# Inverting a chunk's triangular matrix in a hybrid decoder layer: 16x16 diagonal blocks by substitution on VectorE, three levels instead of six, two slots for each hop

## The reference

```python
lower = jnp.where(strict, jnp.einsum('bhnid,bhnjd->bhnij', kb, k) * decay, 0.0)
eye = jnp.eye(c, dtype=jnp.float32)
tmat = lax.linalg.triangular_solve(eye + lower, jnp.broadcast_to(eye, lower.shape),
                                   left_side=True, lower=True, unit_diagonal=True)
u = tmat @ vb
w = tmat @ (kb * jnp.exp(g)[..., None])
```

## Time and profile before

| what | value |
|---|---|
| median of 3 runs | 823.94 us (823.16 to 825.99) |
| the profiled execution's own time | 824.77 us |
| its span, first to last instruction | 823.1 us |
| TensorE busy | 807.9 us |
| VectorE busy | 484.0 us |
| ScalarE busy | 410.0 us |
| GpSimd busy | 140.5 us |
| mean granted TensorE clock | 0.995 of full |

### The profile page before, as it was taken

The page is one execution under the profiler, slowest core; times in us unless marked ns, Lnnn a source line. Parts: engine busy times, 40 slices in busy tenths (PEclk is TensorE's granted clock), DMA queues, the critical chain, the costliest instruction groups (busy, mean ns, idle before and its releaser), DMA issues.

```text
span 823.1 us, 12564 instructions
## 1 busy us (share of the span) xinstructions
PE 807.9 (98%) x3859; PEld 666.3 (81%) x3859; DVE 484.0 (59%) x794; ACT 410.0 (50%) x641; POOL 140.5 (17%) x222
## 2 busy tenths in 40 slices
PE   8899999999999999999999999999999999999996
PEld 7788887888888888878888888888888888888874
DVE  4666448555754664585458456654764566765563
ACT  4564545545544555454545545454555563444441
POOL 9112112110211021102112110211031100001120
PEclk9999999999999999999999999999999999999999
DMA  8856565565656455746565564556454566578652
GB/s 210 231 138 190 139 186 156 172 174 158 178 151 179 129 178 153 193 138 180 152 178 162 153 186 136 180 160 185 137 171 137 183 212 187 182 237 282 196 155 102
DMA packets 179207, 142.15 MB, mean 173 GB/s; under 512 B 10880, under 2 KB 144240, under 8 KB 179056
## 3 DMA queue, kind: packets, MB, share of 16 engines
q1 hardware_dynamic: 179184, 141.85, 59.6%
HBM read 139.72 MB, written 2.10 MB: 172 GB/s over the span
## 4 chain that ended last, share of the span: by engine, by line
PE 91%; DVE 3%; issue 2%; SPq 2%; DMA 1%; ACT 0%; DVEq 0%; POOLq 0%; POOL 0%; ACTq 0%
PE pj L497 27%; PE pj L499 27%; PE pj L498 26%; PE dn_ps L569 1%; PE dn_ps L574 1%; PE dn_ps L552 1%; PE dn_ps L539 1%; DVE w_lo L1011 1%; SPq L269 1%; DVE decay L1100 1%; PE dn_ps L564 1%; DMA w_raw<-in_w_in_dram 1%; SPq L274 1%; SPq L252 1%; PE mo_ps L547 0%
## 5 line engine op out<-in xcount | busy, mean ns | idle before, releaser
L1011 DVE TENSOR_TENSOR w_lo<-w_raw,w_hi 128x1024 fp32r<-128x1024 f32 x251 | 312.9, 1250 | 179.9 <-ACT w_hi L785 179.0
L497 PE MATMUL pj<-w_hi,xt_hi 128*128 128x512 f32 x860 | 356.9, 415 | 3.2 <-DVE w_lo L1011 3.1
L785 ACT ACTIVATE w_hi<-w_raw 128x1024 fp32r<-128x1024 f32 x251 | 264.3, 1058 | 149.9 <-PE pj L499 132.2
L499 PE MATMUL pj<-w_hi,xt_lo 128*128 128x512 f32 x860 | 338.7, 394 | 0.0
L498 PE MATMUL pj<-w_lo,xt_hi 128*128 128x512 f32 x860 | 336.4, 391 | 0.0
L499 PEld LDWEIGHTS pj<-w_hi,xt_lo 128*128 128x128 f32 x860 | 161.8, 188 | 36.6
L497 PEld LDWEIGHTS pj<-w_hi,xt_hi 128*128 128x128 f32 x860 | 162.4, 189 | 33.3 <-issue 3.8
L498 PEld LDWEIGHTS pj<-w_lo,xt_hi 128*128 128x128 f32 x860 | 162.7, 189 | 27.4
L430 POOL TENSOR_TENSOR xo<-v,own 128x128 f32<-128x128 f32 x48 | 44.6, 929 | 232.9 <-DVE v L1174 231.0
L875 ACT ACTIVATE ysb<-dn_ps 128x128 f32<-128x128 f32 x48 | 13.2, 276 | 63.0 <-PE dn_ps L569 63.0
L1174 DVE TENSOR_TENSOR v<-v,dn_ps 128x128 f32<-128x128 f32 x48 | 13.7, 286 | 45.5 <-PE dn_ps L574 44.6
(11 more groups left out here) (259 smaller groups left out, 766.0 us busy)
## 6 DMA issues: line engine op xcount, KB each, us to landing
w_raw<-in_w_in_dram SPq DMA_DIRECT2D x384, 256.0 KB, 3.1
w_raw<-in_w_out_dram SPq DMA_DIRECT2D x64, 256.0 KB, 3.7
w_raw<-in_w_branch_a_dram SPq DMA_DIRECT2D x32, 256.0 KB, 3.3
w_raw<-in_w_branch_b_dram SPq DMA_DIRECT2D x32, 256.0 KB, 3.5
gate<-in_x_dram SPq DMA_DIRECT2D x8, 256.0 KB, 5.2
gate<-in_x_dram SPq DMA_DIRECT2D x4, 512.0 KB, 7.2
gate<-in_final_norm_gain_dram SPq DMA_DIRECT2D x1, 1024.0 KB, 8.7
out_dram<-gate SPq DMA_DIRECT2D x1, 768.0 KB, 3.7
```

The source lines that it names most:

```text
L497: pe.matmul(bank[:, t, :], hi[:, k, tok], w_hi[:, slot, cs], start=(k == 0), stop=False)
L499: mm = pe.matmul(bank[:, t, :], lo[:, k, tok], w_hi[:, slot, cs], start=False, stop=(k == kt_all - 1))
L785: act.activation(w_hi[:, slot, :], w_raw[:, slot, :], ACT.Copy).then_inc(hi_ready, 1)
L1011: dve.tensor_tensor(w_lo[:, slot, :], w_raw[:, slot, :], w_hi[:, slot, :].bitcast(F32), ALU.subtract).then_inc(lo_ready, 1)
```

## The change

The levels start at 16x16 blocks. The inverse of the eight 16x16 diagonal blocks is now made by substitution on DVE. At slot 26 DVE keeps the diagonal blocks of `-w` (`diag`), gathers them into 16 columns (`wc`) and spreads them over 256 columns (`spread`). At slot 28 TensorE multiplies that with a matrix of block ones (line 594 and on of the changed kernel), and ACT copies the product to `lrep`, which gives every partition its block's rows. From slot 29 to 34 DVE does 15 steps for each of two chains (`xs[:, 0]` for the lower blocks, `xs[:, 1]` for the upper), then `xc` and `v`. Three levels follow, with two slots for a hop. POOL makes all level masks `mt` at once, with the start of `xs` behind the first. The softmax's scores move from slot 37 to 36 (M_QK), the transposes of `ya` from 47 to 46 (M_YT). Of the constants, those for the blocks are new. A scratch output of `S_KK` goes to `xf` instead of `v0`.

```diff
-LEVELS = 6
+LEVELS = 3
+BS = 16
...
-S_Y = [31, 35, 39, 43, 47, 51]
-S_XY = [y + 1 for y in S_Y]
-S_XT = [y - 1 for y in S_Y]
+S_SPREAD = 28
+
+SUB = {29: (0, 3), 30: (3, 5), 31: (5, 8), 32: (8, 10), 33: (10, 13), 34: (13, 15)}
+S_V = 34
+S_XT, S_Y, S_XY = [36, 42, 48], [38, 44, 50], [40, 46, 52]
...
-M_TURN, M_QK, M_EXP, M_PT, M_PV, M_YT = 34, 37, 40, 42, 44, 47
+M_TURN, M_QK, M_EXP, M_PT, M_PV, M_YT = 34, 36, 40, 42, 44, 46
...
                 for n in range(LEVELS):
                     pool.tensor_tensor(mt[:, n, :], w[:, :], levels[:, n, :], ALU.mult).then_inc(mt_ready, 1)
+                    if n == 0:
+                        pool.tensor_copy(xs[:, :, :], delta[:, None, :].to_broadcast([P, 2, BS])).then_inc(xs_set, 1)
+                for n in range(LEVELS):
                     pool.wait_ge(v_ready, (LEVELS + 1) * h + n + 1)
                     pool.tensor_tensor(xo[:, :], v[:, :], own[:, n, :], ALU.mult).then_inc(xo_ready, 1)
...
+                if s == S_SPREAD:
+                    pe.wait_ge(spread_ready, h + 1)
+                    pe.wait_ge(kk_ready, 3 * (h + 1))
+                    pe.matmul(A[:, 0:BS * BS], blocks[:, :], spread[:, :, :].rearrange("p j i -> p (j i)"),
+                              start=True, stop=True).then_inc(spread_done, 1)
...
+                if s == S_SPREAD:
+                    act.wait_ge(spread_done, h + 1)
+                    if not first:
+                        act.wait_ge(sub_step, 2 * (BS - 1) * h)
+                    act.activation(lrep[:, :, :].rearrange("p j i -> p (j i)"), A[:, 0:BS * BS], ACT.Copy).then_inc(lrep_ready, 1)
...
-                    dve.tensor_tensor(v0[:, :], w[:, :], neg1[:, :], ALU.mult).then_inc(v0_ready, 1)
-                    dve.wait_ge(v0_ready, h + 1)
-                    if not first:
-                        dve.wait_ge(xf_ready, T * h)
-                    dve.tensor_tensor(v[:, :], v0[:, :], ident[:, :], ALU.add).then_inc(v_ready, 1)
-
+                    dve.tensor_tensor(diag[:, :], w[:, :], blocks_neg[:, :], ALU.mult).then_inc(diag_ready, 1)
+                    dve.wait_ge(diag_ready, h + 1)
+                    if not first:
+                        dve.wait_ge(spread_done, h)
+                    dve.tensor_reduce(wc[:, :], diag[:, :].rearrange("p (b i) -> p i b", i=BS), AX_X, ALU.add).then_inc(wc_ready, 1)
+                    dve.wait_ge(wc_ready, h + 1)
+                    dve.tensor_tensor(spread[:, :, :], wc[:, None, :].to_broadcast([P, BS, BS]),
+                                      delta[:, :, None].to_broadcast([P, BS, BS]), ALU.mult).then_inc(spread_ready, 1)
...
+                if s in SUB:
+                    if SUB[s][0] == 0:
+                        dve.wait_ge(lrep_ready, h + 1)
+                        dve.wait_ge(xs_set, h + 1)
+                    for n in range(*SUB[s]):
+
+                        for t, j, later_rows in ((0, n, slice(n + 1, BS)), (1, BS - 1 - n, slice(0, BS - 1 - n))):
+                            if n:
+                                dve.wait_ge(sub_step, 2 * (BS - 1) * h + 2 * n - 1 + t)
+                            dve.scalar_tensor_tensor(out=xs[:, t, later_rows], in0=lrep[:, j, later_rows],
+                                                     scalar=xs[:, t, j:j + 1], in1=xs[:, t, later_rows],
+                                                     op0=ALU.mult, op1=ALU.add).then_inc(sub_step, 1)
+                if s == S_V:
+                    dve.wait_ge(sub_step, 2 * (BS - 1) * (h + 1))
+                    dve.tensor_tensor(xc[:, :], xs[:, 0, :], xs[:, 1, :], ALU.add).then_inc(xc_ready, 1)
+                    dve.wait_ge(xc_ready, h + 1)
+                    if not first:
+                        dve.wait_ge(xf_ready, T * h)
+                    dve.tensor_tensor(v[:, :].rearrange("p (b i) -> p b i", i=BS), xc[:, None, :].to_broadcast([P, P // BS, BS]),
+                                      blocks_half[:, :].rearrange("p (b i) -> p b i", i=BS), ALU.mult).then_inc(v_ready, 1)
```

More of the change, by code:

```diff
@@ L102, in build @@
         earlier = sb("earlier", [P, P])
-        neg1 = sb("neg1", [P, P])
+        blocks = sb("blocks", [P, P])
+        blocks_neg = sb("blocks_neg", [P, P])
+        blocks_half = sb("blocks_half", [P, P])
+        delta = sb("delta", [P, BS])
         levels = sb("levels", [P, LEVELS, P])
@@ L135, in build @@
         v = sb("v", [P, P])
-        v0 = sb("v0", [P, P])
+        diag = sb("diag", [P, P])
+        wc = sb("wc", [P, BS])
+        spread = sb("spread", [P, BS, BS])
+        lrep = sb("lrep", [P, BS, BS])
+        xs = sb("xs", [P, 2, BS])
+        xc = sb("xc", [P, BS])
         xe = sb("xe", [P, P])
@@ L194, in build @@
         vb_ready, kk_done, kk_ready, mt_ready = sem("vb_ready"), sem("kk_done"), sem("kk_ready"), sem("mt_ready")
-        w_ready, v0_ready, v_ready, vT_done = sem("w_ready"), sem("v0_ready"), sem("v_ready"), sem("vT_done")
+        w_ready, v_ready, vT_done = sem("w_ready"), sem("v_ready"), sem("vT_done")
+        diag_ready, wc_ready, spread_ready, spread_done, lrep_ready = (sem(n) for n in (
+            "diag_ready", "wc_ready", "spread_ready", "spread_done", "lrep_ready"))
+        xs_set, sub_step, xc_ready = sem("xs_set"), sem("sub_step"), sem("xc_ready")
         xe_ready, xo_ready, xf_ready = sem("xe_ready"), sem("xo_ready"), sem("xf_ready")
@@ L364, in _ @@
             for n in range(LEVELS):
-                s = 2 << n
-                blocks = own[:, n, :].rearrange("p (b c) -> p b c", c=s)
-                pool.affine_select(out=blocks, in_=ones[:, :].rearrange("p (b c) -> p b c", c=s), compare_op=ALU.is_ge,
+                s = BS << n
+                every = own[:, n, :].rearrange("p (b c) -> p b c", c=s)
+                pool.affine_select(out=every, in_=ones[:, :].rearrange("p (b c) -> p b c", c=s), compare_op=ALU.is_ge,
                                    fill=0.0, base=0, pattern=[[-s, P // s], [0, s]],
@@ L370, in _ @@
                 pool.wait_ge(const_step, done + 1)
-                pool.affine_select(out=blocks, in_=blocks, compare_op=ALU.is_ge, fill=0.0, base=s - 1,
+                pool.affine_select(out=every, in_=every, compare_op=ALU.is_ge, fill=0.0, base=s - 1,
                                    pattern=[[s, P // s], [0, s]], channel_multiplier=-1).then_inc(const_step, 1)
@@ L374, in _ @@
             pool.wait_ge(const_step, done)
-            pool.tensor_tensor(neg1[:, :], ident[:, :], own[:, 0, :], ALU.subtract).then_inc(const_step, 1)
+            pool.tensor_copy(blocks[:, :], own[:, 0, :]).then_inc(const_step, 1)
+            pool.tensor_tensor(blocks_neg[:, :], ones[:, :], own[:, 0, :], ALU.subtract).then_inc(const_step, 1)
+            pool.tensor_tensor(blocks_half[:, :], ident[:, :], half[:, 2:3].to_broadcast([P, P]), ALU.mult).then_inc(const_step, 1)
+            pool.tensor_tensor(diag[:, 0:64], ident[:, 0:64], ident[:, 64:128], ALU.add).then_inc(const_step, 1)
+            done += 4
+            pool.wait_ge(const_step, done)
+            pool.tensor_tensor(blocks_neg[:, :], blocks_neg[:, :], ones[:, :], ALU.subtract).then_inc(const_step, 1)
+            pool.tensor_tensor(blocks_half[:, :], own[:, 0, :], blocks_half[:, :], ALU.subtract).then_inc(const_step, 1)
+            pool.tensor_tensor(diag[:, 64:96], diag[:, 0:32], diag[:, 32:64], ALU.add).then_inc(const_step, 1)
+            done += 3
+            pool.wait_ge(const_step, done)
+            pool.tensor_tensor(delta[:, :], diag[:, 64:80], diag[:, 80:96], ALU.add).then_inc(const_step, 1)
+            done += 1
             for n in range(LEVELS):
@@ L379, in _ @@
                 pool.tensor_tensor(levels[:, n, :], wider, own[:, n, :], ALU.subtract).then_inc(const_step, 1)
-            done += 1 + LEVELS
+            done += LEVELS
             pool.wait_ge(const_step, done)
             for n in range(LEVELS):
-                s = 2 << n
+                s = BS << n
                 pairs = own[:, n, :].rearrange("p (b e c) -> p b e c", e=2, c=s)
@@ L568, in dn_step @@
                     pe.wait_ge(mt_ready, LEVELS * h + n + 1)
+                    if n == 0:
+                        pe.wait_ge(lrep_ready, h + 1)
                     pe.matmul(A[:, 0:P], mt[:, n, :], xe[:, :], start=True, stop=True).then_inc(y_done, 1)
@@ L1129, in dn_step @@
                     for t, gram in ((0, A[:, K00 * P:(K00 + 1) * P]), (1, B[:, P:2 * P])):
-                        dve.tensor_tensor_reduce(v0[:, :] if t else xe[:, :], gram, ident[:, :], 1.0, 0.0, ALU.mult, ALU.add,
+                        dve.tensor_tensor_reduce(xf[:, 1, :] if t else xe[:, :], gram, ident[:, :], 1.0, 0.0, ALU.mult, ALU.add,
                                                  ssk[:, t:t + 1]).then_inc(k_squared, 1)
```

## The result

The changed kernel takes 813.62 us (812.41 to 814.37) against 824.97 us, a ratio of 0.9862 with a 95% interval of 0.9841 to 0.9883. The forecast was 814.6 us with 812.3 to 819.0. In a second comparison on one chip it was 813.16 against 824.53 us, 0.9862 (0.9846 to 0.9878).

A forecast was written before the change was run, and what follows sets the result against it. TensorE, busy for 98% of the span, was taken to bound the kernel. Removed levels -13.7, added product +3.4, new waits +0.2 and +0.8 make -9.3 us, so 823.9 becomes 814.6 us, range 812.3 to 819.0.

The forecast's parts named there:

- What bounds the kernel: TensorE, busy 98% of the span: time is the sum of what it issues, and no hop of the inverse is waited for.
- What is removed: Three of six levels in each of 8 heads, 24 x 0.57 = 13.7 us of TensorE (13.2 to 14.2).
- The added product: One 128x256 product a head on TensorE at slot 28, 8 x 0.43 = 3.4 us.
- Step 1: DVE's spread block ready for TensorE at slot 28: slack 0.5 us, only the first head waits, 0.2 us.
- Step 2: ACT's copy to lrep ahead of unit 17's weight conversion: four microseconds of cover before slot 33, no cost.
- Step 3: DVE's 30 substitution steps, 0.1 us each, 3.1 for all; v ready 2.4 us before slot 36 needs it, no cost.
- The point from which it would be the end of the gain: Slower rival: at 0.23 us between substitution steps the gain of 1.3 us a head is used up; chance 0.04.
- Step 5: End of a head: ACT's gate copy releases the next head's unit 0 late by 0.1 us, 0.8 us in all.
- only in other slots: TensorE's other products and the softmax's stay and merely change slots, with no cost counted for the move.
- The sum: All terms together: -13.7 + 3.4 + 0.2 + 0.8 = -9.3 us, giving 814.6 us.

The follow-up runs named there:

- masks behind spread: The changed kernel with POOL's three level masks and the start of xs waiting for the spread multiply; 812.76 us in one run.

## Why the prediction was right, step by step

The mechanism was right; the change of time was forecast as -9.3 us and was -11.35. That the median came within 1.0 us of the forecast 814.6 is in part luck: the forecast started from 823.94, the median of three runs, and the fourth made it 824.97. The gain was 2 us larger than forecast, and most of what follows is about where they are.

- **What bounds the kernel.** Right. Putting the removed matmuls back into the changed kernel takes the gain away; taking them from the kernel before gives 14.7 us alone.
- **What is removed.** 24 x 0.57 = 13.7 us; the three levels left out gave 24 x 0.61 = 14.7. The term was 1.0 us too small: the rows of a product said 0.22 to 0.24, and I took the middle. Products put back cost 0.575 a level, so the other 0.04 belong to levels in their place. Waits are not seen there: in the kernel before TensorE is never idle in front of a level's matmul, and a weight load of one for 0.05 us at most. The cause stays open.
- **The added product.** 3.4 us, and 0.43 a head by its own doubling. Right; in its place slots 28 and 29 are 0.45 us longer than in the run with levels left out and two-slot hops.
- **Step 1.** The reduction took 0.38 for 0.29 and the multiply 0.72 for 0.42, the second by POOL's mask. Spread was done at 441.77, TensorE's weight load came at 442.03: no wait in the loop. In the first head TensorE waited: 66.27 instead of 65.96 for the product, and 0.10 more inside it, 0.4 us against 0.2 forecast. Right, with less slack than said (0.26 for 0.5).
- **Step 2.** The copy to lrep started 0.71 us behind the product for 0.73 forecast, and unit 17's w_lo ended 3.3 us behind it for 3.4. Cover as forecast.
- **Step 3.** The step distance was 0.143 and not 0.10, because I halved a distance of 0.21 seen between other instructions: one of these steps stands 0.26 behind the one that it waits for, and two chains halve that but for 0.01 to 0.02. It cost nothing, since the slack of 2.4 us had to shrink to 1.4 only. The point from which it would be the end of the gain, 0.23, is borne out in kind: at 0.26 the kernel was slower than before, by 0.4%, and an estimate from the lengths of a head in that run and in the changed kernel puts the point at 0.25.
- **Step 5.** The order of times was right to 0.01 us (1.69 for 1.70), the cost was wrong: 0.1 us a head forecast, 0.03 seen, 0.2 us in all. The step that failed is "it is released 0.1 late, and all that TensorE has is queued behind". A weight load is wanted one matmul ahead, but about the first 0.12 us of its delay cost nothing: 0.15 us late (472.17 for 472.02) cost 0.03, 0.24 late (first head, masks behind spread) cost 0.12, 0.53 late (first head of the changed kernel) cost 0.41. What the prediction put at nothing is the move of the softmax's slots itself, "only in other slots": it costs 0.06 us a head, this wait included.
- **The sum.** Per head: -1.84 for the levels, +0.43 for the product, +0.06 for the softmax's slots make -1.35, and -1.46 was measured. Another 0.11 us a head (0.9 us in all) of gain is not accounted for; the distance of the hops gives 0.03 of it, 0.06 stands in slots 8 to 15, and the cause stays open. With the first head's wait the sum is -14.7 + 3.4 + 0.5 - 0.9 + 0.4 = -11.3 against -11.35 measured and -9.3 forecast; since the 0.9 is what was left over, this says only that the length of a head accounts for the median. Of the difference of 2 us, 1.0 is the size of a level, 0.9 that remainder and 0.3 the head's end with the softmax's slots (0.5 for 0.8), less 0.2 for the first head.

Of the rule "The DRAIN you can't avoid" ("VectorE: DVE Perf Modes", the Trainium skill): the steps show 0.221 us each and start 0.143 apart, so instructions do overlap when they wait for the last but one. The section goes on to say that a next instruction that is not held starts earlier, which the prediction left out; these steps fit that sentence. When each waits for the one before, 0.26, there is no overlap, and the advice to count instructions would have been the right one.

## What to carry to other kernels

Where one engine is dense, count what it issues from start to start, and let every other engine's work only pass the question whether it is in time. Moving work from a dense TensorE to VectorE pays here even at 30 small instructions for three levels, so long as independent chains keep them overlapped and the latency fits between the times at which TensorE wants two results. Measure the length of one repeated stretch: it told 0.03 us a head apart where medians scatter by 2 us. And when a forecast lies near the result, compare its terms one by one: here they were off by up to 1.0 us each, and 0.9 us of the gain have a place in part and no cause.

## What the runs showed of the hardware

- An in-place scalar-tensor-tensor of up to 15 columns shows 0.22 us; such instructions start 0.25 to 0.27 us apart when each waits for the one before and 0.13 to 0.145 when each waits for the last but one. The small ones of the kernel before showed 0.21 and 0.07.
- A 128x256 product in full float32 costs TensorE 0.43 us between projection matmuls, its two fp32r parts 0.24 together.
- A weight load that starts 0.15 us late costs the matmuls 0.03, one 0.24 late 0.12, one 0.53 late 0.41: in these three places the delay less 0.12.
- Projection matmuls of 512 columns start 0.22 to 0.24 us apart, and the same stretch of them (slots 8 to 15) takes 12.23 us in one kernel and 12.29 in another.
- A VectorE multiply of two SBUF tiles grows from 0.42 to 0.72 us beside a GpSimd product, and the small instruction behind it from 0.16 to 0.42. A GpSimd product grows from 0.46 to 1.44 us beside a VectorE split of 1.22.
